# Q, K and V weights loaded as pairs of neighbouring column blocks in a float32 decoder kernel

## The reference, cut to what matters

```python
mod = (cond @ mod_w[i] + mod_b[i])[:, None, :]      # cond = silu(c), one row
sh_m, sc_m, g_m, sh_f, sc_f, g_f = jnp.split(mod, N_MOD, axis=-1)
h = x * (1.0 + sc_m) + sh_m
qkv = h @ w_qkv            # (256 x 2048) @ (2048 x 6144)
q, k, v = jnp.split(qkv, 3, axis=-1)
```

## Time and profile before

| | |
|---|---|
| median of 3 executions | 2215.92 us (2215.51 to 2216.18) |
| the profiled execution's own time | 2215.93 us |
| its span in the trace | 2214.2 us |
| PE busy | 2176.4 us, 98% of the span |
| PEld / DVE / ACT / POOL busy | 83% / 79% / 51% / 0% |
| moved by DMA | 650.41 MB, 294 GB/s over the span |
| first 330 us (modulation start, Q, K, V) | 126.80 MB, 384 GB/s |

### The profile page before, as it was taken

The page is one execution under the profiler, slowest core; times in us unless marked ns, Lnnn a source line. Parts: engine busy times, 40 slices in busy tenths (PEclk is TensorE's granted clock), DMA queues, the critical chain, the costliest instruction groups (busy, mean ns, idle before and its releaser), DMA issues.

```text
span 2214.2 us, 27547 instructions
## 1 busy us (share of the span) xinstructions
PE 2176.4 (98%) x10442; PEld 1832.5 (83%) x10442; DVE 1756.4 (79%) x1804; ACT 1125.6 (51%) x1403; POOL 7.8 (0%) x26
## 2 busy tenths in 40 slices
PE   6999999999999999999999999999999999999998
PEld 5999988888788888888888878888888888888886
DVE  7899999977988988999877898667666666665667
ACT  4777785465345435435554433337544543543552
POOL 0000000000000000000000000000000000000000
PEclk9999999999999999999999999999999999999999
DMA  9999998869999999999858988766887787866672
GB/s 354 385 386 396 398 378 304 282 234 331 395 374 325 387 342 323 376 349 313 312 170 309 317 301 288 228 208 209 260 293 236 247 276 230 264 216 190 201 264 99
DMA packets 317043, 650.41 MB, mean 294 GB/s; under 512 B 31840, under 2 KB 63088, under 8 KB 315248
## 3 DMA queue, kind: packets, MB, share of 16 engines
q1 hardware_dynamic: 313568, 634.73, 83.0%
q10 hardware_dynamic: 3344, 13.93, 1.6%
HBM read 623.15 MB, written 2.12 MB: 282 GB/s over the span
## 4 chain that ended last, share of the span: by engine, by line
PE 86%; DVE 6%; DMA 4%; issue 2%; ACT 1%; SPq 1%; DVEq 0%; ACTq 0%
PE bank L1469 25%; PE bank L1471 25%; PE bank L1470 25%; DMA mod_raw<-in_mod_w 3%; PE bank L1459 3%; PE bank L1462 3%; PE bank L1461 3%; DVE w_low L1099 1%; DVE mod_acc L1014 1%; DMA stage<-stage 1%; PE bank L1476 1%; PE bank L1481 1%; PE bank L1477 1%; DMA raw<-in_attn_w_qkv 0%; SPq L577 0%
## 5 line engine op out<-in xcount | busy, mean ns | idle before, releaser
L745 ACT ACTIVATE w_high<-raw 128x1024 fp32r<-128x1024 f32 x752 | 786.6, 1057 | 961.0 <-PE bank L1471 906.1
L1099 DVE TENSOR_TENSOR w_low<-raw,w_high 128x1024 fp32r<-128x1024 f32 x752 | 912.2, 1221 | 352.3 <-ACT w_high L745 351.7
L1469 PE MATMUL bank<-w_high,h_high 128*128 128x512 f32 x1632 | 636.5, 390 | 4.0 <-DVE w_low L1099 4.0
L1470 PE MATMUL bank<-w_low,h_high 128*128 128x512 f32 x1632 | 635.0, 389 | 0.0
L1471 PE MATMUL bank<-w_high,h_low 128*128 128x512 f32 x1632 | 635.0, 389 | 0.0
L1014 DVE SCALAR_TENSOR_TENSOR mod_acc<-mod_raw,cond,mod_acc 128x1024 f32<-128x1024 f32 x345 | 441.8, 1281 | 28.7 <-DMA mod_raw<-in_mod_w 25.9
L1469 PE MATMUL bank<-w_high,hid_high 128*128 128x512 f32 x1048 | 408.3, 390 | 0.9 <-DVE w_low L1099 0.9
L1471 PE MATMUL bank<-w_high,hid_low 128*128 128x512 f32 x1048 | 407.7, 389 | 0.0
L1470 PE MATMUL bank<-w_low,hid_high 128*128 128x512 f32 x1048 | 407.7, 389 | 0.0
L1469 PEld LDWEIGHTS bank<-w_high,h_high 128*128 128x128 f32 x1632 | 306.4, 188 | 69.0 <-issue 3.6
L1471 PEld LDWEIGHTS bank<-w_high,h_low 128*128 128x128 f32 x1632 | 306.4, 188 | 63.7
(11 more groups left out here) (158 smaller groups left out, 1179.1 us busy)
## 6 DMA issues: line engine op xcount, KB each, us to landing
raw<-in_mlp_w SPq DMA_DIRECT2D x512, 512.0 KB, 5.6
mod_raw<-in_mod_w SPq DMA_DIRECT2D x368, 512.0 KB, 8.2
raw<-in_attn_w_qkv SPq DMA_DIRECT2D x96, 512.0 KB, 10.6
raw<-in_conv_w_in SPq DMA_DIRECT2D x96, 512.0 KB, 5.9
stage<-stage SPq DMA_DIRECT2D x176, 128.0 KB, 2.9
raw<-in_attn_w_o SPq DMA_DIRECT2D x32, 512.0 KB, 7.5
raw<-in_conv_w_out SPq DMA_DIRECT2D x32, 512.0 KB, 4.8
mod_raw<-in_mod_w SPq DMA_DIRECT2D x32, 256.0 KB, 6.3
```

The lines of the kernel that those rows point to most:

```text
L745: act.activation(chunk_slots(n)[0], raw[:, n % NCH], ACT.Copy).then_inc(high_done, 1)
L1099: dve.tensor_tensor(low_, raw[:, n % NCH], high.bitcast(F32), ALU.subtract).then_inc(raw_used, 1)
L1469: pe.matmul(dst, high[:, k, c], wh, start=first, stop=False, skip_group_check=True)
L1470: pe.matmul(dst, high[:, k, c], wl, start=False, stop=False, skip_group_check=True)
```

## The change

The 96 loads of 512 KB for Q, K and V become 48 loads of 1 MB. A pair is two neighbouring column blocks of the same 256 rows, so each of its rows is 4 KB instead of 2 KB. The pairs are chunks (0,1), (2,3) to (10,11), and from 12 on (n, n + 2) and (n + 1, n + 3) of each four. The same 32 KB of each partition are now four places of a pair for these loads. `raw_chunk(n)` is the half of the pair that chunk n is; ACT and DVE read it as two runs of 512 elements that lie 1024 elements apart, where they had 1024 in one run. A pair is issued at the step of its first chunk for the first four pairs, and later at the step (second chunk of the pair that had the place) + 8: pair 4 (8,9) at n = 9, pair 5 (10,11) at 11, pair 6 (12,14) at 13, pair 7 (13,15) at 15, pair 8 (16,18) at 17, pair 9 (17,19) at 19, pair 10 (20,22) at 22, pair 11 (21,23) at 23, and so on. ACT waits for the whole pair. The next matrix's first eight chunks wait until the pairs under their slots are used up (`raw_free`). Nothing else moves: the tiles, the orders of ACT, DVE and PE, and the sums are as before.

```diff
+    PAIRED = [(n, n + 1) for n in range(0, 2 * LEADING, 2)]
+    PAIRED += [(n + j, n + j + PART_CH) for n in range(2 * LEADING, len(CHUNKS), 2 * PART_CH) for j in range(PART_CH)]
+    PLACE = {n: (i, half) for i, pair in enumerate(PAIRED) for half, n in enumerate(pair)}
+    SLOT_PAIRS = NCH // 2
+    PAIR_LOAD_AT = {pair[0] if i < SLOT_PAIRS else PAIRED[i - SLOT_PAIRS][1] + NCH: i
+                    for i, pair in enumerate(PAIRED)}
+    def raw_free(n):
+        if len(CHUNKS) <= n < len(CHUNKS) + NCH:
+            return max(n - NCH, PAIRED[n % NCH // 2 - SLOT_PAIRS][1]) + 1
+        return n - NCH + 1
...
+            def load_pair(i, n):
+                v, jj = CHUNKS[PAIRED[i][0]]
+                r, g, _ = VISITS[v]
+                k = r * GT + CK * jj
+                sp_.wait_ge(raw_used, n + 1)
+                sp_.dma_start(raw_pairs[:, i % SLOT_PAIRS], qkv_rows[:, k:k + CK, g * GC:(g + 2) * GC]
+                              ).then_inc(raw_in[i % SLOT_PAIRS * 2], 16)
             def load_chunk(n):
                 if n < N_O:
-                    v, jj = CHUNKS[n]
-                    r, g, _ = VISITS[v]
-                    k = r * GT + CK * jj
-                    src = qkv_rows[:, k:k + CK, g * GC:(g + 1) * GC]
-                else:
-                    rows, k0, col = weights(n // NCH)
-                    k = k0 + CK * (n % NCH)
-                    src = rows[:, k:k + CK, col:col + GC]
-                sp_.wait_ge(raw_used, n + 1)
+                    if n in PAIR_LOAD_AT:
+                        load_pair(PAIR_LOAD_AT[n], n)
+                    return
+                rows, k0, col = weights(n // NCH)
+                k = k0 + CK * (n % NCH)
+                src = rows[:, k:k + CK, col:col + GC]
+                sp_.wait_ge(raw_used, raw_free(n) + CREDIT_RAW)
                 sp_.dma_start(raw[:, n % NCH, :, :], src).then_inc(raw_in[n % NCH], 16)
...
-                act.wait_ge(raw_in[n % NCH], n // NCH * 16 + 16)
+                slot, count = raw_loaded(n)
+                act.wait_ge(raw_in[slot], count)
                 act.wait_ge(chunk_mult, free_after(n) + 1 + CREDIT_SPLIT)
-                act.activation(chunk_slots(n)[0], raw[:, n % NCH], ACT.Copy).then_inc(high_done, 1)
+                act.activation(chunk_slots(n)[0], raw_chunk(n), ACT.Copy).then_inc(high_done, 1)
...
-                dve.tensor_tensor(low_, raw[:, n % NCH], high.bitcast(F32), ALU.subtract).then_inc(raw_used, 1)
+                dve.tensor_tensor(low_, raw_chunk(n), high.bitcast(F32), ALU.subtract).then_inc(raw_used, 1)
```

More of the change, by code:

```diff
@@ L91, in build_trunk, with raw_loaded @@
     QC = QKV * PART_CH
+    PAIRED = [(n, n + 1) for n in range(0, 2 * LEADING, 2)]
[8 more added lines that the diff above has]
+        return n - NCH + 1
+    def raw_loaded(n):
+        if n < len(CHUNKS):
+            i = PLACE[n][0]
+            return i % SLOT_PAIRS * 2, 16 * (i // SLOT_PAIRS + 1)
+        return n % NCH, 16 * (n // NCH + 1 - (n % 2) * (len(PAIRED) // SLOT_PAIRS))
     BANK0 = N_VISITS - W_O
@@ L467, in chunk_slots, with raw_chunk @@
             return w_high[:, slot], w_low[:, slot]
+        raw_pairs = flat(raw[:, :, :, :].rearrange("p s k n -> p s (k n)")).rearrange(
+            "p (d k n) -> p d k n", d=SLOT_PAIRS, k=CK)
+        def raw_chunk(n):
+            if n < N_O:
+                i, half = PLACE[n]
+                return raw_pairs[:, i % SLOT_PAIRS, :, half * GC:(half + 1) * GC]
+            return raw[:, n % NCH]
         y_tok = flat(y[:, :, :]).rearrange("p (t d) -> p t d", t=TT)
```

## The result

The changed kernel takes 2218.99 us (median of 19 executions, 2216.22 to 2223.17) against 2215.92 us before (19 executions, 2214.19 to 2218.95): a ratio of 1.0014, 95% interval 1.0007 to 1.0020. That is 3.1 us or 0.14% slower, within 0.2%; the forecast was 2218.4 us, in a range of 2214.8 to 2221.8. The interval doesn't reach 1, so the loss is real, though it is small. The profiled execution took 2218.62 us with a span of 2216.9, 2.7 more than before.

What follows compares the result with a forecast made beforehand. It took PE as full from 60 to 300 us, with DMA full too but mostly hidden behind PE; a 2.5 us stop ahead of chunk 12, all else costed at nothing, on 2215.93 gave 2218.4 us, range 2214.8 to 2221.8.

Steps and rivals of the forecast that it cites:

- What sets the end: From 60 to 300 us PE and DMA are both full; PE's waits decide, late chunks reaching it through ACT's order.
- The landing of pair 7: Pair 7, at chunk 15's place in the queue, lands at 67.1 us, so `high(13)` starts then instead of at 63.52.
- The saving of 0.15 us a pair: 4 KB rows cut a pair's DMA time from 2.71 to 2.56 us, 7 us over 48 pairs, hidden behind PE.
- the steady lateness: Rival: from chunk 24 on each of 18 groups of four can cost PE 0.3 us, giving 2223.8; chance 0.10.
- Split reads: ACT and DVE reading two runs of 512 elements costs nothing; the bound is a few tens of ns.
- from there on the work is the same: Behind chunk 12 PE is full to 300 us, so its 2.5 us delay stays and nothing gives it back.
- the clock rival: Rival: TensorE's clock falls in the new gap ahead of chunk 12, 2.3 us more, giving 2220.7; chance 0.10.
- chunk 12's start is fixed by a landing: At the start, what PE gains ahead of chunk 12 is idled away there, so it counts for nothing.
- The gain of up to 1 us: At the start, ACT's chain ends 0 to 1 us sooner; a gain only without the stop at chunk 12.
- The idle ahead of chunk 3: At the start, chunk 3 waits about 0.9 us more, while chunk 4's 1.95 us of idling mostly goes.
- The queue doesn't run dry: Behind chunk 12, three or four tile issues come 3.7 us late, but 10 us of queue latency covers that.
- the prediction's 5 us: Pair 9 lands some 5 us after chunk 17 did; counted as nothing, with about 1 us as the bound.

Runs made afterwards that it cites:

- pairs 6 and 7 sooner: Changed kernel with pairs 6 and 7 issued one step earlier, at steps 12 and 14: 2216.03 us against 2216.12 before.
- chunk 13 late: Kernel before with only chunk 13's load moved, to directly ahead of chunk 15: 2218.58 us against 2215.68 before.
- two halves of 2 KB rows: Changed kernel with each pair loaded by two 512 KB DMAs on one semaphore: 2221.94 us against 2215.68 before.
- fillers: Changed kernel with 20 extra matmuls ahead of chunk 12 (2218.55 and, timed again, 2218.60 us), or ahead of chunks 3 and 12 (2218.60 us).
- one filler: Changed kernel with 20 extra matmuls of 256 columns between chunks 11 and 12, into an unread bank: 2218.55 us, timed again 2218.60.

## Why the prediction was right

**What sets the end** was read rightly: PE waits for no chunk itself, and ahead of chunk 12 only by ACT's order. The three profiles of the changed kernel have no wait of PE between 75 and 320 us, and the kernels that move one load (pairs 6 and 7 sooner, chunk 13 late) take the loss away and bring it back.

**The landing of pair 7**, 67.1, was 67.18; chunk 12, 69.15, was 69.26. Part of that accuracy is luck, since the first matmul of that execution came 0.8 us later than before's. Counted from the first matmul, the forecast for `high(13)` is 43.5 us, and the three profiles have 42.7, 43.7 and 44.3; for chunk 12 it is 45.5, and they have 44.8, 45.75 and 46.4 (before: 43.0).

**The saving of 0.15 us a pair**, 2.56 against 2.71, holds up: from 120 to 180 us the DMA engines move 397 GB/s instead of 387, and 386 again with two halves of 2 KB rows, with which pair 7 lands later. From 240 to 300 us they are no longer always full (385 GB/s against 399, share 1.00 against 1.04): they got ahead of PE, as the case against the steady lateness had it. That rival is out. Split reads cost nothing: over Q, K and V alone (24 to 314 us) L778 and L1132 have means of 1047 and 1220 ns, as L745 and L1099 had before.

**The step that was incomplete** is "from there on the work is the same": the clock rival had been given 0.10 and 2.3 us, and it came in two of three profiles behind chunk 12, at 1.6 us. So two of the three took the course of that rival, whose time was 2220.7; that the median is nearer to the forecast's 2218.4 is in part luck.

**The step that was too simple** is "chunk 12's start is fixed by a landing", with what happens ahead of it at nothing. The gain of up to 1 us is there in the first profile only (chunk 11 starts 39.35 us after the first matmul, 40.0 in before, 40.3 and 42.0 in the other two). The idle ahead of chunk 3, forecast at 0.8 + 0.9 = 1.7 us, was 1.8 to 3.0, and in the other two the clock fell there or behind chunk 6. Such a loss isn't idled away ahead of chunk 12, because the landing moves too. SP issues pair 7 behind a tile, and tiles wait for DVE (11 to 13 us in all between 46 and 62 us). In the profile without a fall ahead of chunk 12 it issues the pair 33.5 us after the first matmul and the pair lands at 42.7; with a fall behind chunk 3 it is 34.7 and 43.7, with one behind chunk 6 it is 36.5 and 44.3. The three profiles with fillers have landings at 43.2 and 43.4 (fall behind 3) and 44.4 (behind 6). That the falls put the landing back, by 0.4 to 0.9 and by 1.6 to 1.7 us, is read from these six profiles; no run tried it.

In the stretch to chunk 95 the cost was thus 3.4 to 4.3 us over before's 288.4, not 2.5: chunk 12 later by 1.8, 2.75 and 3.4 us, and 1.6 us of low clock behind it in the first two. The executions' medians have 3.1. Why the medians show less than the profiles isn't settled; single executions of either kernel spread over 3 to 7 us.

**"The queue doesn't run dry"** was wrong, without a price. The modulation tile that was put back was issued at 70.72, and from 73.6 to 76.4 the engines moved only 330 GB/s:

```profile
73.60:76.40 2.80, 2.80 (x24) 2.80 (x24) 2.80 (x3) 1.06 (x1) 0.00 (x0) 0.94 0.96 330
```

`high(17)` came at 81.28, where the prediction's 5 us behind the 73.88 of before would be 78.9. PE, 4 us late by then, did not notice; nor did it in the two profiles with one filler, where the clock had stayed at chunk 12.

## What to carry to other kernels

A bigger DMA in a full queue is paid for by whoever is first in it: count for each chunk what stands ahead of it in the queue now, find the one whose place moves back most, and look at what its consumer does next in its order, for that is what stops the bottleneck engine. Keep the place of the earliest user when merging loads: one step sooner for two pairs gave back all that the change had cost. And price a new idle of TensorE with what may follow it at the low clock: behind the idles of 2.3 us here it was 1.6 us more. Don't count a loss ahead of a late load as absorbed either, before you have asked whether the load's own issue waits for engines that the loss puts back.

## What the runs showed of the hardware

After an idle of PE of about 2 us and more in the middle of dense matmuls, the granted clock fell to the 1.2 GHz level in 14 of the 21 cases (idles of 1.86 to 3.14 us) that the 14 profiles above have between 30 and 1290 us, each time for about 3.4 us, and some 1.6 us were lost by it behind chunk 12. It is not a matter of length alone: the clock stayed after six idles of 1.94 to 2.15 us (ahead of chunks 3 and 4, and once near 1287 us) and after one of 2.35 us ahead of chunk 6, and it fell after 1.86 us in another execution. No idle under 1.8 us had a fall behind it. The Trainium skill (TensorE: Matmul & The Clock Gate, Part 1) has the gate follow how busy PE has recently been; the trace agrees in kind.
